# Head norms of a two-layer hybrid decoder, their roots and reciprocals taken on tokens by heads

## What is computed

```python
def l2norm(x, eps=1e-6):
    return x * lax.rsqrt(jnp.sum(x * x, axis=-1, keepdims=True) + eps)
# gated DeltaNet, inputs
q = l2norm(q.reshape(b, s, h, dk)) * (dk ** -0.5)
k = l2norm(k.reshape(b, s, h, dk))
# gated DeltaNet, output
o = rms_norm(o, norm_w) * jax.nn.silu(z.astype(F32).reshape(b, s, h, dv))
# retention, output
mu = jnp.mean(o, axis=-1, keepdims=True)
var = jnp.mean(jnp.square(o - mu), axis=-1, keepdims=True)
on = ((o - mu) * lax.rsqrt(var + NORM_EPS)).reshape(bsz, s, h * dv) * norm_w.astype(F32)
return (jax.nn.silu(g.astype(F32)) * on).astype(dtype)
```

## Time and profile before

| | |
|---|---|
| time, median of 3 runs (lowest to highest) | 1333.64 us (1330.99 to 1337.56) |
| the profiled execution | 1334.75 us, of which the span of the trace 1333.0 us |
| TensorE busy (matmuls) | 98% of the span |
| VectorE, ScalarE, GpSimd busy | 70%, 49%, 17% |
| RECIPROCAL on 128 x 512 | 8 of them (4 a layer), 3.34 to 3.35 us each |
| time in which TensorE waited for another engine or a DMA | 25 us in 29 waits |

### The profile page before, as it was taken

How to read it: one execution, slowest core, us unless ns; L and a number is a source line. 1 busy time by engine, 2 the same in 40 slices (tenths; PEclk the granted TensorE clock), 3 DMA queues, 4 the chain that set the end, 5 groups by cost and what they waited for, 6 DMA issues and landing times. The chain is left out here.

```text
span 1333.0 us, 27445 instructions
## 1 busy us (share of the span) xinstructions
PE 1301.6 (98%) x11728; PEld 1266.9 (95%) x11728; DVE 930.6 (70%) x1435; ACT 659.6 (49%) x953; POOL 230.0 (17%) x183
## 2 busy tenths in 40 slices
PE   8999999999999999999999999999999999999997
PEld 8899999998888999999999999999978899999997
DVE  5788675896857866666658885567788588566654
ACT  6544646753234464444455446477422455544542
POOL 1000011004834610000100000100166263000000
PEclk9999999999999999999999999999999999999999
DMA  5655564544132556556545555545422345455562
GB/s 196 239 170 198 188 195 140 173 155 132 65 127 95 168 174 197 187 188 228 190 159 190 190 184 195 176 152 166 159 96 73 120 141 185 160 186 187 181 216 91
DMA packets 61465, 220.24 MB, mean 165 GB/s; under 512 B 6944, under 2 KB 7200, under 8 KB 60960
## 3 DMA queue, kind: packets, MB, share of 16 engines
q1 hardware_dynamic: 61344, 218.50, 49.6%
HBM read 217.42 MB, written 1.05 MB: 164 GB/s over the span
## 5 line engine op out<-in xcount | busy, mean ns | idle before, releaser
L447 PE MATMUL bank<-xh,whi 128*128 128x256 f32 x2256 | 638.4, 283 | 8.6 <-DVE wlo L1303 7.5
L448 PE MATMUL bank<-xl,whi 128*128 128x256 f32 x2256 | 631.2, 280 | 0.0
L449 PE MATMUL bank<-xh,wlo 128*128 128x256 f32 x2256 | 630.9, 280 | 0.0
L1303 DVE TENSOR_TENSOR wlo<-raw,whi 128x1024 fp32r<-128x1024 f32 (+1 forms) x384 | 469.2, 1245 | 229.3 <-ACT whi L905 227.9
L905 ACT ACTIVATE whi<-raw 128x1024 fp32r<-128x1024 f32 (+1 forms) x414 | 419.8, 1035 | 176.6 <-PE bank L449 98.1
L447 PEld LDWEIGHTS bank<-xh,whi 128*128 128x128 f32 x2256 | 425.1, 188 | 15.5 <-issue 8.4
L448 PEld LDWEIGHTS bank<-xl,whi 128*128 128x128 f32 x2256 | 425.2, 188 | 0.2
L449 PEld LDWEIGHTS bank<-xh,wlo 128*128 128x128 f32 x2256 | 425.0, 188 | 0.0
L449 PE MATMUL bank<-hh,wlo 128*128 128x256 f32 x704 | 197.0, 280 | 0.0
L447 PE MATMUL bank<-hh,whi 128*128 128x256 f32 x704 | 196.7, 279 | 0.0
L448 PE MATMUL bank<-hl,whi 128*128 128x256 f32 x704 | 196.6, 279 | 0.0
(11 more groups left out here) (366 smaller groups left out, 1445.8 us busy)
## 6 DMA issues: line engine op xcount, KB each, us to landing
raw<-weights SPq DMA_DIRECT2D x350, 512.0 KB, 3.8
raw<-weights SPq DMA_DIRECT2D x64, 448.0 KB, 4.0
cst<-consts SPq DMA_DIRECT2D x1, 1088.0 KB, 8.2
par<-params SPq DMA_DIRECT2D x1, 1072.5 KB, 8.7
par<-params SPq DMA_DIRECT2D x1, 1060.5 KB, 9.5
x<-x_in SPq DMA_DIRECT2D x2, 512.0 KB, 7.7
y_out<-ret SPq DMA_DIRECT2D x4, 256.0 KB, 2.3
ropec<-positions SPq DMA_DIRECT2D x1, 128.0 KB, 8.7
```

The lines of the kernel that those rows point to most:

```text
L447: mm(out, w[0], a[0], start=start, stop=False)
L448: mm(out, w[0], a[1], start=False, stop=False)
L449: return mm(out, w[1], a[0], start=False, stop=stop)
L1303: V.tensor_tensor(slot(wlo, i), slot(raw, i), r32(slot(whi, i)), ALU.subtract).then_inc(S("low_dve"), 1)
```

## The change

The mean, the root and the reciprocal are formed in another layout: tokens on the partitions, and one column for each of (128-token block, head). `head_cols` is 32 columns of `small`: 16 for q and k, 8 for the DeltaNet output, 8 for the retention output.

- `head_means` takes the squares themselves as the stationary side (128 features x 128 tokens) and two columns of `bo` (one per head of the tile) as the moving side: four matmuls of two columns each per tensor of 256 features.
- ScalarE takes the roots of 16, 8 and 8 columns in place of 512 each, and VectorE the reciprocals likewise.
- `over_heads` brings them back to the features: the column of a head, broadcast to 64 columns, is the stationary side and the identity (128 x 128) the moving one; the result goes to the 64 partitions of the head. Eight matmuls for each of four units (`l2qb`, `l2kb`, `gsb`, `rv2b`). VectorE then multiplies q, k and the two outputs with the PSUM bank directly.
- TensorE waits for the reciprocals (`heads_inv`) in front of `over_heads`: at the first place between the transposes of `rows` and `rv`, at the second between the second half of g13 and g14.

```diff
 SIDE
-          ("l2q", "act"), ("l2k", "act"), ("rowt", "act"), ("eb", "act"),
+          ("l2", "act"), ("rowt", "act"), ("l2qb", "dve"), ("l2kb", "dve"), ("eb", "act"),
 ...
-           ("gs", "act"), ("rv2", "act")])
+           ("gs", "act"), ("rv2", "act"), ("gsb", "dve"), ("rv2b", "dve")])
 tensor_layer
-            for unit, q0, ev in (("l2q", 0, 1), ("l2k", 2, 2)):
-                pe.wait_ge(S("qk_sq"), ev)
+            def head_means(ps, at, src):
+                for t in range(2):
+                    for j in range(2):
+                        c = at + 4 * t + 2 * j
+                        last = mm(ps[:, c:c + 2], src[:, t, j * P:(j + 1) * P], bo.rearrange("p (h c) -> p h c", h=2)[:, :, 0], start=True, stop=True)
+                return last
+            def over_heads(unit, at):
                 ps = side_bank(unit)
                 for t in range(2):
-                    last = mm(ps[:, t * SEQ:(t + 1) * SEQ], bo, mx_sq[:, q0 + t, :], start=True, stop=True)
+                    for j in range(2):
+                        for hp in range(2):
+                            c = at + 4 * t + 2 * j + hp
+                            last = mm(ps[64 * hp:64 * hp + 64, t * SEQ + j * P:t * SEQ + (j + 1) * P], head_cols[:, c:c + 1].to_broadcast([P, 64]), ident, start=True, stop=True)
                 last.then_inc(S("side"), 1)
+            ps = side_bank("l2")
+            for q0 in (0, 2):
+                pe.wait_ge(S("qk_sq"), q0 // 2 + 1)
+                last = head_means(ps, 4 * q0, mx_sq[:, q0:q0 + 2, :])
+            last.then_inc(S("side"), 1)
             pair("rg")
 ... (rowt)
+            pe.wait_ge(S("heads_inv"), 1)
+            over_heads("l2qb", 0)
+            over_heads("l2kb", 8)
 ... (rv, g0)
-            pe.wait_ge(S("k_normed"), 1)
+            pe.wait_ge(S("side_dve"), side.taken("l2kb"))
 ...
             half("g13", 0)
             pe.wait_ge(S("go_sq"), 1)
-            means("gs", tmpD)
+            head_means(side_bank("gs"), 16, tmpD).then_inc(S("side"), 1)
             pe.wait_ge(S("ro_sq"), 1)
-            means("rv2", tmpC)
+            head_means(side_bank("rv2"), 24, tmpC).then_inc(S("side"), 1)
             half("g13", 1)
+            pe.wait_ge(S("heads_inv"), 2)
+            over_heads("gsb", 16)
+            over_heads("rv2b", 24)
             gate(14)
 scalar_layer
-            for unit, dst in (("l2q", mx_sq[:, 0:2, :]), ("l2k", mx_sq[:, 2:4, :])):
-                A(dst, halves(side.bank(unit)[:]), ACT.Sqrt, scale=float(DH), bias=eps_col).then_inc(S("side_act"), 1)
+            A(head_cols[:, 0:16], side.bank("l2")[:, 0:16], ACT.Sqrt, scale=float(DH), bias=eps_col).then_inc(S("side_act"), 1)
 ... (gs and rv2 likewise, 8 columns each)
 vector_layer
-            V.reciprocal(mx_sq[:, 0:2, :], mx_sq[:, 0:2, :])
+            V.reciprocal(head_cols[:, 0:16], head_cols[:, 0:16]).then_inc(S("heads_inv"), 1)
             ahead("rv")
-            link(V.reciprocal(mx_sq[:, 2:4, :], mx_sq[:, 2:4, :]))
-            V.scalar_tensor_tensor(qkv[:, 0:2, :], qkv[:, 0:2, :], 0.5 * DH ** -0.5, mx_sq[:, 0:2, :], ALU.mult, ALU.mult)
+            dve.wait_ge(S("side"), side.ready("l2qb"))
+            V.scalar_tensor_tensor(qkv[:, 0:2, :], qkv[:, 0:2, :], 0.5 * DH ** -0.5, halves(side.bank("l2qb")[:]), ALU.mult, ALU.mult)
 ... (k likewise)
             dve.wait_ge(S("side_act"), side.taken("gs"))
-            link(V.reciprocal(tmpD, tmpD))
-            link(V.tensor_tensor(go, go, tmpD, ALU.mult))
+            link(V.reciprocal(head_cols[:, 16:24], head_cols[:, 16:24]))
+            dve.wait_ge(S("side_act"), side.taken("rv2"))
+            V.reciprocal(head_cols[:, 24:32], head_cols[:, 24:32]).then_inc(S("heads_inv"), 1)
+            dve.wait_ge(S("side"), side.ready("gsb"))
+            V.tensor_tensor(go, go, halves(side.bank("gsb")[:]), ALU.mult).then_inc(S("side_dve"), 1)
 ... (gate, branch 0, g15.0's remainder, as before)
-            link(V.reciprocal(tmpC, tmpC))
-            link(V.tensor_tensor(tmpB, tmpB, tmpC, ALU.mult))
+            dve.wait_ge(S("side"), side.ready("rv2b"))
+            V.tensor_tensor(tmpB, tmpB, halves(side.bank("rv2b")[:]), ALU.mult).then_inc(S("side_dve"), 1)
```

More of the change, by code:

```diff
@@ L348, in trunk @@
         one_col = cst_("one")
+        head_cols = small[:, 72:104]
         nega = small[:, 151:152]
@@ L1109, in scalar_layer @@
             ahead("rg")
-            for unit, dst in (("l2q", mx_sq[:, 0:2, :]), ("l2k", mx_sq[:, 2:4, :])):
-                act.wait_ge(S("side"), side.ready(unit))
-                A(dst, halves(side.bank(unit)[:]), ACT.Sqrt, scale=float(DH), bias=eps_col).then_inc(S("side_act"), 1)
+            act.wait_ge(S("side"), side.ready("l2"))
+            A(head_cols[:, 0:16], side.bank("l2")[:, 0:16], ACT.Sqrt, scale=float(DH), bias=eps_col).then_inc(S("side_act"), 1)
             act.wait_ge(S("lru_q"), 1)
@@ L1183, in scalar_layer @@
             act.wait_ge(S("side"), side.ready("gs"))
-            A(tmpD, halves(side.bank("gs")[:]), ACT.Sqrt, bias=eps_col).then_inc(S("side_act"), 1)
+            A(head_cols[:, 16:24], side.bank("gs")[:, 16:24], ACT.Sqrt, bias=eps_col).then_inc(S("side_act"), 1)
             act.wait_ge(S("side"), side.ready("rv2"))
-            A(tmpC, halves(side.bank("rv2")[:]), ACT.Sqrt, bias=eps_col).then_inc(S("side_act"), 1)
+            A(head_cols[:, 24:32], side.bank("rv2")[:, 24:32], ACT.Sqrt, bias=eps_col).then_inc(S("side_act"), 1)
             act.wait_ge(S("s5_done"), 1)
@@ L1617, in vector_layer @@
             link(last)
-            dve.wait_ge(S("side_act"), side.taken("l2k"))
-            V.reciprocal(mx_sq[:, 0:2, :], mx_sq[:, 0:2, :])
+            dve.wait_ge(S("side_act"), side.taken("l2"))
+            V.reciprocal(head_cols[:, 0:16], head_cols[:, 0:16]).then_inc(S("heads_inv"), 1)
             ahead("rv")
-            link(V.reciprocal(mx_sq[:, 2:4, :], mx_sq[:, 2:4, :]))
-            V.scalar_tensor_tensor(qkv[:, 0:2, :], qkv[:, 0:2, :], 0.5 * DH ** -0.5, mx_sq[:, 0:2, :], ALU.mult, ALU.mult)
-            V.scalar_tensor_tensor(qkv[:, 2:4, :], qkv[:, 2:4, :], 0.5, mx_sq[:, 2:4, :], ALU.mult, ALU.mult).then_inc(S("k_normed"), 1)
-            dve.wait_ge(S("k_normed"), 1)
+            dve.wait_ge(S("side"), side.ready("l2qb"))
+            V.scalar_tensor_tensor(qkv[:, 0:2, :], qkv[:, 0:2, :], 0.5 * DH ** -0.5, halves(side.bank("l2qb")[:]), ALU.mult, ALU.mult).then_inc(S("side_dve"), 1)
+            dve.wait_ge(S("side"), side.ready("l2kb"))
+            V.scalar_tensor_tensor(qkv[:, 2:4, :], qkv[:, 2:4, :], 0.5, halves(side.bank("l2kb")[:]), ALU.mult, ALU.mult).then_inc(S("side_dve"), 1)
+            dve.wait_ge(S("side_dve"), side.taken("l2kb"))
             split_to(piece_at("g1.0") + 1)
@@ L1800, in vector_layer @@
             dve.wait_ge(S("side_act"), side.taken("gs"))
-            link(V.reciprocal(tmpD, tmpD))
-            link(V.tensor_tensor(go, go, tmpD, ALU.mult))
+            link(V.reciprocal(head_cols[:, 16:24], head_cols[:, 16:24]))
[3 more added lines that the diff above has]
+            V.tensor_tensor(go, go, halves(side.bank("gsb")[:]), ALU.mult).then_inc(S("side_dve"), 1)
+            dve.wait_ge(S("side_dve"), side.taken("gsb"))
             link(V.scalar_tensor_tensor(go, go, gnh, zz, ALU.mult, ALU.mult))
```

6 lines of the change are left out of this document (3 added, 3 removed).

## The result

| | |
|---|---|
| time after, median of 6 runs (lowest to highest) | 1343.76 us (1342.66 to 1346.44) |
| time before, beside it, median of 6 runs | 1334.31 us (1330.99 to 1337.56) |
| ratio, 95% interval | 1.0075 (1.0058 to 1.0092) |
| the profiled execution after | 1345.84 us, span 1344.1 us |

What follows compares the result with a forecast made beforehand. The prediction took TensorE, busy 98% of the span, as the bound. 3.35 us at the first place and 1.3 at the second, in two layers, made 9.3 us more: 1343.0 us on the median, range 1338 to 1349.

Steps and rivals of the forecast that it cites:

- What bounds the kernel: TensorE, busy 98% of the span; taking VectorE's work away pays only where a remainder or branch comes late behind a reciprocal.
- The means: On TensorE at each place, sixteen short records replace eight: 0.0 to +0.3 us, taken as +0.1.
- over_heads: On TensorE at each place, 32 added records with column halves side by side: 1.9 us, ends 1.7 and 3.5.
- Rival (a): In over_heads the column halves do not overlap: 3.5 us each, 1347.7 us in all; chance 0.12.
- The wait at the first place: TensorE waits for the small reciprocal, behind line 1614 and two scans on VectorE: 1.35 us, bounds 1.1 and 2.3.
- The second place: Means and over_heads added, g15.0's wait 0.85 in place of 1.15, branch 3's 0.4 gone: +1.3 us a layer.
- rival (c): The new waits of 1.35 us could each bring a clock fall: +1.8 us each, up to 1346.6; chance 0.08.
- The sum: Both places, both layers: (3.35 + 1.3) x 2 = 9.3 us, giving 1343.0 us on the median.

Runs made afterwards that it cites:

- the kernel with one half at a time: The changed kernel with over_heads' loops turned round, so each unit's matmuls write first the lower 64 partitions, then the upper; 1347.09 us, ratio to before 1.0096.
- the edit alone: The changed kernel with the first place put back to its form of before, so only the norms of the two outputs are changed; 1335.20 us, ratio 1.0012.
- the kernel with the exponential: The kernel before, with ScalarE forming the second place's reciprocal roots by logarithm and exponential in place of VectorE's two reciprocals there; 1336.81 us, ratio 1.0026.
- the first experiment: The changed kernel with VectorE's 16-column reciprocal at the first place moved ahead of the recurrent branch's product and two scans; 1339.64 us, ratio to before 1.0046.

## Why the prediction was right

**What bounds the kernel.** Held: TensorE's records rose by 8.7 us of busy time and the time followed, while VectorE's 23.4 us bought nothing outside the second place. With the reciprocals left out altogether, of the two places only the second got shorter. (I had forecast 26 us less on VectorE; the branch's remainder of 428.19, for one, took 2.77 us in place of 0.69, sitting out GpSimd.)

**The means: +0.1 us a place.** Held: 1.54 us before for eight records up to the next matmul, 1.70 after for sixteen, +0.16.

**over_heads: 1.9 us a place.** Held to 0.01 us, but in part by luck. I had 3.5 us for the same work in one half and a gain of 1.6 from working in two; the runs show 2.49 and 0.6. The two errors cancel, because I took the total in proportion to the neighbour row of alternating halves. The 0.216 us a record that the 3.5 came from is not 1.54 / 8, which is 0.19, as I wrote; it is the step of the second place's means (four records from 418.04 to 418.91). Rival (a) priced the same loss at 4.7 us; the kernel with one half at a time shows 1.2 us in its stretches.

**The wait at the first place: 1.35 us.** The mechanism was right (the reciprocal behind the scans behind ScalarE's second root), the size was low. In layer 0 it is 1.41 idle, 1.66 from where the transposes end. The step that was off: I let line 1114's root move up by the 0.95 us that the first root got shorter; it moved up 0.74 against the means (6.93 us behind them in the earlier trace rows, 6.19 now), because the weight copy ahead of it landed 0.24 us later. In layer 1 the same copy is 1.0 us later still, and the wait is 2.42, above my upper bound of 2.3. A wait for a DMA stood in ScalarE's queue ahead of the new critical path, and I had not named it.

**The second place: +1.3 us.** The first layer has +1.15, the edit alone +1.15 and +1.17. The turn-taking came out as walked: cast first, then GpSimd, the branch's remainder, GpSimd, g15.0's remainder, with TensorE waiting 0.51 idle (0.67 lost, 0.85 forecast), and branch 3's wait gone. Layer 1 has 0.77 us more; the larger part of it is the wait of 0.47 us idle for the late weight piece of 1098.16.

**The clock, rival (c).** The new waits brought no fall of the clock: it stays at 1.00 behind both, though one is 2.42 us long. But the falls move from run to run, as the section on the hardware tells.

**The sum.** 9.3 us forecast, 11.3 in the four stretches of the profiled execution, 7.7 to 12.3 by the ratio. Of the 2.0 us missing, 1.8 are what layer 1 has over layer 0 at the two places, where the rows show late weight pieces. By the medians the change costs 9.45 us and the forecast was 9.3. That this is so close is luck: the interval is 2.3 us to either side, and the profiled execution has 2.0 us that I had not foreseen.

## What to carry to other kernels

Work taken off an engine that is not full is worth only the waits that it causes, and those can be added up beforehand; here 1.75 us a layer stood against 2.1 us and more at each place on the full engine. Before work is moved to the full engine, look at the order around those waits: 1.6 us of products moved into an idle stretch took away both waits of the second place and made the kernel faster than before (ratio 0.9965). When VectorE and GpSimd exclude each other, GpSimd can work beside a long instruction that doesn't exclude it, and taking that instruction out can make the chain later, as in the kernel with the exponential.

## What the runs showed of the hardware

**VectorE and GpSimd take strict turns.** When both have instructions waiting, each gets one in turn, whatever its length. In the twelve traces 626 VectorE instructions with all operands in SBUF (sums, products, casts) start during one of GpSimd's elementwise instructions; every one ends only behind it, and none sits out a second. In the kernel with the exponential five short instructions of VectorE sat out five of GpSimd's, 1.7 to 2.6 us each. Reciprocals and products with a PSUM input ran beside GpSimd undisturbed in every trace. The Trainium skill ("SBUF — State Buffer", Who interferes with whom) has the exclusive port pair; the trace agrees, and adds the alternation, which decides how much a queue of short instructions loses.

**The cost of a small reciprocal.** 0.20 us for 8 columns and 0.25 for 16, against 3.35 for 512: by these numbers 0.0063 us a column and some 0.15 fixed.

**Not every long wait brings a fall of the clock.** In each of the twelve profiles the granted clock falls to 0.50, the lower of its two levels, at one to four places, mostly for 3.4 us, which costs 1.7 us, twice for 6.8; one more fall comes in each at the end of the program, when TensorE has little or nothing left. Past the first 40 us each fall but that last one begins in, or less than 2 us behind, a wait of TensorE of 1.3 to 3.3 us. The same wait brings a fall in one kernel and none in the next; what decides it, these runs don't show. Behind the wait of 2.0 us near 333 us, the changed kernel and the one of the first experiment (windows: length, busy us by engine, granted clock, DMA share, GB/s):

```profile
334.00:336.00 2.00, 2.00 (x17) 0.98 (x17) 1.86 (x4) 0.00 (x0) 1.38 (x2) 0.50 0.03 10
```

```profile
334.00:336.00 2.00, 2.00 (x18) 2.00 (x19) 1.82 (x4) 1.33 (x2) 1.95 (x2) 1.00 0.03 8
```

These falls are part of the 9 us between the lowest and the highest execution of the kernel before (1329.19 to 1338.41 us in 24): its four executions with a mean granted clock of 0.993 took 1334.2 to 1338.4 us, the four with 0.996 took 1329.2 to 1334.0. They are a reason to compare stretches of two traces and not their spans.
